# Due times between the experts' rows, set anew for the first half's sums

## What is computed

```python
# first block (cut)
h = h + mixers(rms_norm(h)) @ w_out
idx, gates = peer_route(hn @ w_q, sub_keys)          # 8 heads x 16 of 16384 experts, for each token
act = gelu(einsum("chkd,cd->chk", take(u, idx), xc))
out = einsum("chk,chkd->cd", act * gates, take(v, idx))
x = rms_norm(h + out)
# second block
x = x + 0.5 * swiglu(rms_norm(x), gate, up, down)    # hidden width 2816
proj = rms_norm(x) @ w_in                            # latents, fox q, k, v, gates
y_fox, y_mla = two causal attentions, 8 heads each
x = x + (sigmoid(g_mla) * (y_mla @ w_mla) + sigmoid(g_fox) * (y_fox @ w_fox)) @ w_o
x = x + 0.5 * swiglu(rms_norm(x), gate2, up2, down2)
```

## Time and profile before

| | |
|---|---|
| Median of 3 runs | 2482.41 us (2480.25 to 2482.93) |
| The profiled execution | 2480.95 us |
| Its span, first to last instruction | 2479.1 us |
| Granted TensorE clock, mean | 0.932 |
| DMA: bytes, mean | 760.89 MB, 307 GB/s |
| Busy: PE, DVE, ACT, POOL | 85%, 74%, 48%, 31% |

### The profile page before, as it was taken

The page is one execution under the profiler, slowest core; times in us unless marked ns, Lnnn a source line. Parts: engine busy times, 40 slices in busy tenths (PEclk is TensorE's granted clock), DMA queues, the critical chain, the costliest instruction groups (busy, mean ns, idle before and its releaser), DMA issues.

```text
span 2479.1 us, 28622 instructions
## 1 busy us (share of the span) xinstructions
PE 2111.2 (85%) x9508; PEld 1500.0 (61%) x9508; DVE 1833.3 (74%) x3372; ACT 1180.2 (48%) x3776; POOL 760.6 (31%) x634
## 2 busy tenths in 40 slices
PE   6987898988877777999684578699949999999999
PEld 6965443443222225884343466488529988798997
DVE  6985676868888888887898987776576656567564
ACT  5214556555666664442455554433234436344443
POOL 0001444454555553232465643433220001100000
PEclk9988999999999998999795699899979999999999
DMA  5211999999999998999999999999984544124553
GB/s 210 72 68 58 382 415 421 417 413 421 421 421 420 415 417 346 387 419 398 379 417 353 363 414 365 396 397 421 386 355 170 187 167 167 69 86 155 186 187 136
DMA packets 107460, 760.89 MB, mean 307 GB/s; under 512 B 12064, under 2 KB 12832, under 8 KB 16432
## 3 DMA queue, kind: packets, MB, share of 16 engines
q0 software_dynamic: 73728, 536.90, 53.2%
q1 hardware_dynamic: 33584, 222.15, 23.7%
HBM read 756.91 MB, written 2.10 MB: 306 GB/s over the span
## 4 chain that ended last, share of the span: by engine, by line
PE 44%; DVE 9%; DMA 4%; issue 3%; ACT 1%; POOL 1%; DVEq 0%; ACTq 0%; POOLq 0%
PE bank L582 43%; DVE resid L1062 4%; DMA pair<-in_uv,idx 4%; DVE pair L1728 2%; PE bank L1019 0%; DVE half L1056 0%; DVE tmp L1056 0%; POOL smalls L2373 0%; PE bank L892 0%; POOL pair L2424 0%; DVE smalls L1384 0%; PE bank L825 0%; ACT half L1813 0%; DVE smalls L1470 0%; ACT frow L1813 0%
## 5 line engine op out<-in xcount | busy, mean ns | idle before, releaser
L2424 POOL DMA_INDIRECT pair<-in_uv,idx x512 | 649.6, 1269 | 874.8 <-DVE resid L1062 556.5
L1813 ACT ACTIVATE smalls<-smalls 128x1 f32<-128x1 f32 x2058 | 540.5, 286 | 665.1 <-DVE smalls L1728 647.0
L1728 DVE CUSTOM_DVE_ANT_0 pair<-pair,hn 128x1024 f32<-128x1024 f32 x512 | 624.1, 1220 | 155.4 <-DMA pair<-in_uv,idx 153.8
L582 PE MATMUL bank<-pair,diag 128*128 128x512 f32 x928 | 460.8, 629 | 118.2 <-ACT diag L1813 117.3
L582 PEld LDWEIGHTS bank<-pair,diag 128*128 128x128 f32 x928 | 169.3, 195 | 390.9 <-ACT diag L1813 245.9
L582 PE MATMUL bank<-ft,raw 128*128 128x256 f32 x1664 | 371.8, 387 | 12.0 <-DVE ft L1056 12.0
L1062 DVE SCALAR_TENSOR_TENSOR resid<-pair,smalls,resid 128x1024 f32<-128x1024 f32 x280 | 358.7, 1281 | 0.9 <-DVE resid L1062 0.5
L582 PEld LDWEIGHTS bank<-ft,raw 128*128 128x128 f32 x1664 | 323.1, 195 | 56.6 <-issue 12.5
L1056 DVE TENSOR_TENSOR half<-raw,half 128x1024 fp32r<-128x1024 f32 (+1 forms) x204 | 235.6, 1194 | 124.4 <-ACT half L1813 124.3
L1813 ACT ACTIVATE half<-raw 128x1024 fp32r<-128x1024 f32 (+1 forms) x204 | 199.4, 1025 | 129.0 <-PE bank L582 128.9
L582 PE MATMUL bank<-ft_hi,half 128*128 128x256 f32 x960 | 178.0, 286 | 2.6 <-DVE ft_early L1056 1.5
(11 more groups left out here) (285 smaller groups left out, 2949.8 us busy)
## 6 DMA issues: line engine op xcount, KB each, us to landing
raw<-in_wts SPq DMA_DIRECT2D x196, 1024.0 KB, 6.0
pair<-in_uv,idx POOLq DMA_INDIRECT x512, 11.1
raw<-in_wts SPq DMA_DIRECT2D x10, 512.0 KB, 6.1
raw<-in_wts SPq DMA_DIRECT2D x4, 720.0 KB, 6.3
resid<-in_x SPq DMA_DIRECT2D x4, 512.0 KB, 6.2
out<-resid SPq DMA_DIRECT2D x8, 256.0 KB, 7.5
raw<-in_wts SPq DMA_DIRECT2D x2, 768.0 KB, 6.4
rowt<-in_rows SPq DMA_DIRECT2D x1, 1076.0 KB, 12.1
```

The source lines that it names most:

```text
L582: return e.matmul(o, a, b, start=start, stop=stop)
L1728: e.tensor_tensor_reduce(b[:, 0:1024], b[:, 0:1024], HN[i // 128], 1.0, 0.0, ALU.mult, ALU.add, actv[:, i % 8:i % 8 + 1]).then_inc(dotted, 1)
L1813: return e.activation(o, i, f, **kw)
L2424: e.indirect_dma_start(pair[i % NPAIR], None, uv, bass.IndirectOffsetOnAxis(ap=idx[:, n % SLOTS, k:k + 1], axis=0)).then_inc(pairs_in[i % ...
```

## The change

`Plan.add` takes a tuple of times, one for each use, beside one time for all. With it both tiles of a column half are given nearly the same due time (36 and 2 us instead of 19 and 19 for `down`, 10.5 and 3.5 instead of 7 and 7 for `fq`, `fk`, `fv` and `wo`, 7.5 and 2.5 instead of 5 and 5 for `lat`). The first `up` use of an ffn gets 12 us instead of 7, each `fin` 4 instead of 2. Attention's steps n = 32 to 37, which all had block 31's due time, get 2.5 us more each. `PACE` gives some rows more of the plan clock. No instruction is added, removed or altered; only the places of chain A's steps between the rows, on DVE, ACT and POOL, move. The order on PE and on SP is as before.

```diff
@@ -95,7 +95,7 @@
 START_ROW = 264
 
 
-PACE = ((64, 3.85), (25, 3.3), (28, 2.1), (36, 2.85), (22, 2.6), (64, 3.85), (PAIRS, 2.6))
+PACE = ((64, 3.9), (25, 3.3), (28, 2.1), (36, 3.05), (22, 2.6), (64, 3.9), (PAIRS, 2.6))
 
 
 def clock(row):
@@ -140,11 +140,13 @@
 
     def add(self, stage, banks, us=0.0, told=True):
 
+
+        each = us if isinstance(us, tuple) else (us,) * len(banks)
         n = sum(1 for k in self.uses if k[0] == stage)
         for j, b in enumerate(banks):
             self.fills[b] += told
             self.outs[b] += 1
-            self.clock += us
+            self.clock += each[j]
             self.uses[stage, n + j] = Use(b, self.outs[b] - 1, self.fills[b], self.outs[b], self.clock)
 
     def ring(self, stage, n, us=0.0):
@@ -193,16 +195,17 @@
             p.clock += 8.0
             p.ring(f"norm{f}{x}", 4, 1.5)
             if x == "A":
-                p.ring(f"up{f}{x}", 22, 7.0)
+                p.ring(f"up{f}{x}", 22, (12.0,) + (7.0,) * 21)
             else:
                 for stage, n in (("up", 1), ("rate", 1), ("up", 21)):
                     p.ring(f"{stage}{f}{x}", n, 7.0)
-            p.ring(f"down{f}{x}", 4, 19.0)
+            p.ring(f"down{f}{x}", 4, (36.0, 2.0, 36.0, 2.0))
 
         ffn(1)
         p.clock += 8.0
-        for stage, n, us in (("norm_m", 4, 1.5), ("lat", 2, 5.0), ("fq", 2, 7.0), ("ratem", x == "B", 0.0), ("fk", 2, 7.0),
-                             ("cum", 1, 3.0), ("fv", 2, 7.0), ("tfq", 4, 1.0), ("tfk", 4, 2.0), ("tlat", 2, 1.0)):
+        for stage, n, us in (("norm_m", 4, 1.5), ("lat", 2, (7.5, 2.5)), ("fq", 2, (10.5, 3.5)), ("ratem", x == "B", 0.0),
+                             ("fk", 2, (10.5, 3.5)),
+                             ("cum", 1, 3.0), ("fv", 2, (10.5, 3.5)), ("tfq", 4, 1.0), ("tfk", 4, 2.0), ("tlat", 2, 1.0)):
             p.ring(stage + x, n, us)
         p.add("gate" + x, [4] if x == "A" else [5, 5], 6.0)
         p.add("look" + x, [0, 1] * 8, 3.3)
@@ -211,12 +214,12 @@
         p.add("prep" + x, [6, 7] * 8)
         for blk in range(4):
             p.add("o" + x, [4 + blk % 2], told=False)
-            p.add("fin" + x, [4 + blk % 2], 2.0)
+            p.add("fin" + x, [4 + blk % 2], 4.0)
             if blk in (1, 2):
                 p.add("gate" + x, [3 + blk])
         p.add("gate" + x, [6, 7, 6, 7, 6] if x == "A" else [6, 7, 6, 7])
         p.at = 0
-        for stage, n, us in (("br", 16, 1.8), ("wo", 4, 7.0)):
+        for stage, n, us in (("br", 16, 1.8), ("wo", 4, (10.5, 3.5, 10.5, 3.5))):
             p.ring(stage + x, n, us)
         ffn(2)
     return p
@@ -534,6 +537,10 @@
 
         def when(stage, n):
             return B[stage, n].when
+
+        def when_block(p, n):
+
+            return when("look" + p, min(n, 31)) + 2.5 * max(n - 31, 0)
 
 
         def loads(e):
@@ -1463,7 +1470,7 @@
             def attention(p):
                 t0, nth = T0[p], NTH[p]
                 for n in range(38):
-                    yield when("look" + p, min(n, 31))
+                    yield when_block(p, n)
                     if n < 32:
                         t, h, a = t0 + n % 16 // 8, n % 8, n // 8 % 2
                         o, _ = filled(e, "look" + p, n)
```

## The result

The changed kernel takes 2455.51 us (median of 6 runs, 2451.38 to 2463.06), the kernel before 2482.67 (6 runs, 2477.7 to 2486.1). The ratio is 0.9899, 95% interval 0.9878 to 0.9919: 20 to 30 us faster. The profiled execution is one of 2454.35 us, its span 2452.6 us.

The account below looks back on a forecast made before the run. The prediction took holes in the DMA transfers before row 511, left by DVE's waits, as the bound. Its terms summed to 11.0 us, taking the profiled 2480.95 to 2470.0, or 2471.4 as median; range 2460 to 2484.

Parts of the forecast that it names:

- up2A: First up steps of half A's second ffn: one row later shortens DVE's 5.58 us wait; 1.5 of 6.6 us won.
- the drain: Attention's steps 32 to 37, spread over rows: last ym wait shrinks from 11.24 to about 3.7 us; 4.5 us won.
- new stalls: Rows come up to 8 us earlier against PE, so some later step stands; 2 us lost, between 0 and 8.
- the start: First up1A use moves from row 270 to 271; 0 to 5 us, counted as 0.
- down1A: First ffn's down sums in half A: both stalls go and the 3.3 us hole nearly closes; 3.0 us won.
- `lat` to `fv`: Latents and the steps behind them: half of DVE's 5.33 us wait stays; 1.0 of a 5.9 us hole won.
- attention's second half denser: Second scores take 30 rows instead of 33, the same DVE work where DMA is full; 1 us lost.
- down2A: Second ffn's down sums in half A: no stall or a few us; the whole 4.0 us hole closes.
- What bounds the kernel: Before row 511, time is won only where DMA's holes close, at DVE's waits, not where an engine stops waiting.
- rival A: DVE's backlog is the cost: holes at 1200 to 1240 and 1310 to 1400 lose another 8 us; 2463, chance 0.25.
- Rivals B and C: B: stalls move, 4 us won, 2478, chance 0.15. C: PE limits attention's second half, 7 us lost, 2489, chance 0.10.
- The ceiling of the transfers: 421 GB/s taken as full; by the skill's 358 no holes would close in most of the stretch, leaving 2481.

Follow-up runs that it names:

- u_drain: Changed kernel with attention's steps 32 to 37 put back at block 31's due time; 2459.8 us, ratio 0.9911 to the kernel before.
- ym_pace: Changed kernel with half A's ym scaled one attention step later and the old PACE; 2454.66 us, ratio 0.9883 to the kernel before.

## Why the prediction was wrong in its size

The cause that it gave was right: time was won where waits of DVE, and with them holes of the transfers, went. The step that failed is the size of the terms. The largest error is `up2A`, 1.5 us taken where 6.0 went (4.3 by the second profile); then the drain, 4.5 for 8.3 (6.3), its remaining wait forecast at 3.7 us where none for PE was left; then 2 us charged for new stalls, of which none was found, and the start, put at nothing, which gave 2.5.

Term by term, with the terms of the prediction's sum and what the holes of the profiles before and after differ by, with the changed kernel's second profile beside it:

| term | predicted, us | found, us | second profile |
|---|---|---|---|
| `down1A`, rows 312 to 330 | 3.0 | 4.7 | 4.8 |
| `lat` to `fv`, rows 330 to 346 | 1.0 | 2.8 | 3.1 |
| attention's second half denser (found: rows 346 to 412) | -1.0 | -1.7 | -0.8 |
| drain, rows 412 to 424 | 4.5 | 8.3 | 6.3 |
| `up2A`, rows 444 to 452 | 1.5 | 6.0 | 4.3 |
| `down2A`, rows 488 to 505 | 4.0 | 5.4 | 5.4 |
| start, rows 264 to 312 | 0 | 2.5 | 2.5 |
| new stalls (found: the rows between) | -2.0 | -0.1 | -0.3 |
| sum | 11.0 | 27.9 | 25.3 |

*What bounds the kernel*: supported. From 1620 to 1780 us the transfers run at 419 and 421 GB/s while DVE waits 4.14 us several times over, without a hole; where a long wait went, the hole behind it went, and where it was put back, the hole came back.

*down1A and down2A*: right in kind, with waits near the forecast (none at the first `down1A` sum; 5.86 us at the first `down2A` sum, where I said none or a few and named 5 us as the limit). I counted their holes in windows of fixed times that cut them: 3.3 and 4.0 us against 4.9 and 5.4 from row to row. The sum was charged with the smaller.

*The drain*: what failed is the remaining wait of 3.7 us, and with it the 4.5 us taken of a hole counted at 6.3, which is 8.3 from row to row. ACT's copy and PE's work at this place after the change:

```profile
1479.92 0.38 ACT L1820 ACTIVATE pta<-bank 128x256 f32<-128x256 f32 x1
...
1481.17 3.69 PE L589 MATMUL bank<-ft,raw 128*128 128x256 f32 x16
...
1485.31 3.62 PE L589 MATMUL bank<-ft,raw 128*128 128x256 f32 x16
...
1488.77 1.00 PE L589 MATMUL bank<-vmA,pta 128*128 128x64 f32 x8
```

Copy to last sums is 9.9 us and not 11.5: the two gate halves took 3.69 and 3.62 us, where the earlier trace rows has one of 4.81. I had taken PE's pace from a place where it had just stood for 5.29 us and ran partly at the lower of its two clock levels (1.2 GHz):

```profile
1490.00:1492.00 2.00, 2.00 (x7) 1.64 (x6) 0.00 (x0) 1.11 (x3) 0.00 (x0) 0.50 1.00 414
...
1494.00:1500.00 6.00, 5.79 (x35) 5.15 (x33) 0.12 (x1) 1.22 (x3) 0.00 (x0) 1.00 0.60 239
```

Now PE stands 3.12 us before the last scores' work, and the granted clock from 1480 to 1510 is 1.00. And DVE comes with row 417 at 1486.60, after waiting 1.92 us for the row itself.

*up2A*: the worst sized term. I had one row of DVE's wait (5.58 us at 1603.67). The next step stood too, in the kernel before:

```profile
1610.58 0.42 DVE L1056 TENSOR_TENSOR hidden<-fsg,bank 128x256 f32<-128x256 f32 x1 [4.14 <-ACT fsg L1813]
```

and after the change the two are:

```profile
1590.71 0.42 DVE L1063 TENSOR_TENSOR hidden<-fsg,bank 128x256 f32<-128x256 f32 x1 [2.57 <-ACT fsg L1820]
...
1597.61 0.42 DVE L1063 TENSOR_TENSOR hidden<-fsg,bank 128x256 f32<-128x256 f32 x1 [1.80 <-ACT fsg L1820]
```

5.58 + 4.14 us in two rows that follow each other, with rows between them that only give the buffers back once they are through, against 2.57 + 1.80. In the 14 profiles the hole over rows 444 to 452 is 7.1 to 7.3 us where the second wait is 4.14 and 3.3 or less where it is 1.80. I weighed the first wait against the bounds 0 and 6.6 and took a value near the lower end because "part of the hole is the norm's wait for rows"; the late first `up` alone closes 5.1 of the 7.3 us, so that part was small.

*The start*: I gave no reason for 0. DVE's wait for the first `up1A` products was 5.68 us (at 972.10) and is 2.82 (at 976.06). The runs put the gain on the late first `up`: the missing time over rows 264 to 312 is 12.4 us with this part alone, 16.4 and 16.7 with the others alone.

*The latents*: DVE's wait stays, it even grew, from 5.33 to 6.54 us, and yet 2.8 of the 4.7 us at these rows went, where I had made the gain hang on half of the wait going. DVE's timeline after the change:

```profile
1203.86 1.23 DVE L1735 CUSTOM_DVE_ANT_0 pair<-pair,hn 128x1024 f32<-128x1024 f32 x1 [1.93 <-DMA pair<-in_uv,idx]
...
1207.58 1.23 DVE L1735 CUSTOM_DVE_ANT_0 pair<-pair,hn 128x1024 f32<-128x1024 f32 x1 [1.28 <-DMA pair<-in_uv,idx]
...
1230.65 0.18 DVE L1063 TENSOR_TENSOR smalls<-lat,rowt 128x16 f32<-128x16 f32 x1 [6.54 <-ACT lat L1820]
```

DVE waits for rows at 1203.86 and 1207.58: it has caught up. In the kernel before no row from 328 to 338 is waited for. There the hole looks like this:

```profile
1212.00:1226.56 14.56, 9.53 (x31) 6.64 (x30) 14.56 (x20) 5.83 (x26) 10.07 (x8) 0.63 0.84 311
...
1226.56:1231.90 5.34, 5.34 (x18) 3.24 (x17) 0.01 (x2) 1.97 (x7) 1.75 (x2) 1.00 0.95 361
```

DVE's wait for the latents begins at 1226.56. The 14.6 us before it miss 14.56 x 110/421 = 3.8 us of the 4.7, the wait itself 5.34 x 60/421 = 0.8. So the wait was cheap before, as it is after, and what went lay in front of it. Either the down part alone (4.7 to 2.9 us) or the late first `up` alone (to 2.6, with the wait at the first `down1A` sum at 12.10 us) takes most of it away; with the down part undone 4.2 us are there. That fits rival A in part (a backlog has a price, and these rows were one of the two places it named), but the second of these runs has the long stall and hardly the hole, so the cause of this term stays open. From 1310 to 1400, where A put most of its 8 us, nothing changed. Why no new stall showed is open too.

*Rivals B and C*: the stalls didn't move on, and no `look` step waits for PE in the second half. The charge for the denser half has no support: 1.7 and 0.8 us more are missing over rows 346 to 412, but as much with the old `PACE` (1.6).

*The ceiling of the transfers*: 420 and 421 GB/s stand in four of the windows above, one of them 160 us long, as the sum assumed. The Trainium skill (DMA: Bandwidth & Descriptors, section Where 436 GB/s comes from) says that for transfers between HBM and SBUF the HBM side binds, at about 358 GB/s; the traces of both kernels are above that for this one core, at 419 and 421 GB/s for 160 us.

*The range*: I gave the two down terms their whole holes, the drain two thirds, `lat` and `up2A` less than a quarter, and took off 2 us for stalls that I had not found in any row. The upper bounds of all terms together (3.3 + 5.9 + 6.3 + 6.6 + 4.0 = 26 us, 2455 in terms of the profiled execution, which measured 2454.35) stood in my own first list, and the range ended at 2460. That they come so near the 26.5 us found is partly luck: the fixed windows undercounted four of the holes, the latents' hole did not close whole, and the start was not in the list.

## What to carry to other kernels

Where a shared resource is full nearly always, list its holes first and sum them between two marks of the program, not between two times; that sum, and not the waits, is what a change of order can win. It says where time goes, not why: the cause of a hole is shown by removing the wait that stands at it, and by putting it back. If each hole has a cause that goes, take all of it. A wait costs what the buffers ahead of it don't cover: 9.73 us at the third `down2A` sum had transfers of 412 to 434 GB/s right through it (1812 to 1822 us) and cost nothing, 17.02 us at the first cost 5.4, and two waits close behind each other (5.58 and 4.14 us) cost 7.3 together. Two sums that share their operands come together; give them one due time (shown here for the down stages; for the other pairs the runs don't decide).

## What the runs showed of the hardware

From 980 to 1150 us the DMA share is 1.00 in both kernels at only 405 GB/s, where other full stretches have 421; 6.5 of the 38.8 us "missing" after the change are that. No run tells why.

Executions of the same kernel spread by 12 us (2451.38 to 2463.06) where the kernel before spreads by 8, and the two profiles of the changed kernel differ by 1.7 to 2.0 us each in the holes at rows 412 to 424 and 444 to 452: a few stalls lie at the edge of what seven buffers cover. But these two executions took the same time to 0.4 us, and much of the spread lies elsewhere: over all profiles row 264 begins between 943.0 and 948.3 us, and from row 511 to the end it takes 622.7 to 630.7 us, both outside the rows between which the steps were moved.

In the profile with 630.7 (`u_drain`) the granted clock is 0.66 from 2100 to 2120 us, in the one with 630.3 (`ym_pace`) 0.75, in the changed kernel's 1.00; what sets it there no run tells. A difference of a few microseconds between single executions is therefore no evidence; the missing time of the stretch is the better measure.
